# Gate and up chunks of a mixture-of-experts kernel: two row tiles of each matrix, formed side by side

## The reference

```python
def run_block(args):
    xb, e = args                       # up to 128 rows that chose expert e
    return (jax.nn.silu(xb @ w_gate[e]) * (xb @ w_up[e])) @ w_down[e]
# w_gate, w_up: (32, 1024, 512); w_down: (32, 512, 1024); two experts are chosen for each row
```

## Time and profile before

| | |
|---|---|
| median of 3 runs | 1684.39 us (1683.79 to 1686.82) |
| the profiled execution, span | 1682.9 us |
| what lies around its span (median less span) | 1.5 us |
| PE busy in the span | 96% |
| first matmul of expert 0 | 1070.8 us |
| last matmul of the experts | 1643.8 us |
| the end after it (last scatters, final norm, stores) | 39 us |

### The profile page before, as it was taken

The page is one execution under the profiler, slowest core; times in us unless marked ns, Lnnn a source line. Parts: engine busy times, 40 slices in busy tenths (PEclk is TensorE's granted clock), DMA queues, the critical chain, the costliest instruction groups (busy, mean ns, idle before and its releaser), DMA issues.

```text
span 1682.9 us, 26202 instructions
## 1 busy us (share of the span) xinstructions
PE 1613.2 (96%) x9427; PEld 1470.9 (87%) x9427; DVE 1104.4 (66%) x1967; ACT 845.3 (50%) x1234; POOL 231.8 (14%) x245
## 2 busy tenths in 40 slices
PE   5999999999999999999999999799999999999992
PEld 4999999999999999999999887688888888877781
DVE  5332588888887232114214676898998998888893
ACT  6011366666665321112112211678878778778783
POOL 1111011110110000000000111322122122232310
PEclk9999999999999999999999999799999999999996
DMA  5252111111112111131113712999999999999966
GB/s 151 72 137 79 55 51 51 50 49 39 50 50 88 30 39 50 50 137 52 50 50 126 291 71 82 357 393 379 370 377 376 380 375 379 369 373 370 361 222 224
DMA packets 131857, 305.30 MB, mean 181 GB/s; under 512 B 30404, under 2 KB 92080, under 8 KB 106936
## 3 DMA queue, kind: packets, MB, share of 16 engines
q1 hardware_dynamic: 115415, 267.76, 43.3%
q0 software_dynamic: 16384, 36.76, 7.5%
HBM read 282.81 MB, written 40.41 MB: 192 GB/s over the span
## 4 chain that ended last, share of the span: by engine, by line
PE 88%; DMA 6%; DVE 3%; issue 1%; ACT 1%; SPq 0%; DVEq 0%; POOLq 0%; ACTq 0%
PE bank L725 10%; PE bank L727 9%; PE bank L726 9%; PE bank L1071 8%; PE bank L1059 6%; PE bank L1061 6%; PE bank L1060 6%; PE bank L871 5%; PE bank L873 5%; PE bank L872 5%; DMA e_raw<-in_w_e_gate_dram 5%; PE bank L1019 2%; PE bank L1021 2%; PE bank L1023 2%; PE bank L832 2%; PE bank L1048 1%
## 5 line engine op out<-in xcount | busy, mean ns | idle before, releaser
L1967 DVE TENSOR_TENSOR e_lo<-e_raw,e_hi 128x2048 fp32r<-128x2048 f32 x192 | 433.4, 2288 | 55.4 <-ACT e_hi L1378 52.5
L1378 ACT ACTIVATE e_hi<-e_raw 128x2048 fp32r<-128x2048 f32 x192 | 364.5, 1920 | 50.0 <-DMA e_raw<-in_w_e_gate_dram 20.0
L1167 ACT ACTIVATE w_hi<-w_raw 128x1024 fp32r<-128x1024 f32 x68 | 71.6, 1054 | 325.5 <-DMA w_raw<-in_w_in_dram 182.2
L1493 DVE TENSOR_TENSOR w_lo<-w_raw,w_hi 128x1024 fp32r<-128x1024 f32 x68 | 83.2, 1223 | 203.4 <-ACT w_hi L1167 203.4
L1059 PE MATMUL bank<-e_hi,xT_hi 128*128 128x512 f32 x512 | 205.4, 401 | 3.4 <-DVE xT_lo L1978 3.4
L725 PE MATMUL bank<-h_hi,w_hi 128*128 128x344 f32 x624 | 202.5, 324 | 1.1 <-DVE h_lo L1512 1.1
L1061 PE MATMUL bank<-e_hi,xT_lo 128*128 128x512 f32 x512 | 201.5, 394 | 0.0
L1060 PE MATMUL bank<-e_lo,xT_hi 128*128 128x512 f32 x512 | 201.3, 393 | 0.0
L726 PE MATMUL bank<-h_lo,w_hi 128*128 128x344 f32 x624 | 199.6, 320 | 0.0
L727 PE MATMUL bank<-h_hi,w_lo 128*128 128x344 f32 x624 | 199.6, 320 | 0.0
L871 PE MATMUL bank<-h_hi,w_hi 128*128 128x344 f32 x576 | 190.2, 330 | 0.0
(11 more groups left out here) (351 smaller groups left out, 3164.3 us busy)
## 6 DMA issues: line engine op xcount, KB each, us to landing
e_raw<-in_w_e_gate_dram SPq DMA_DIRECT2D x64, 1024.0 KB, 19.9
e_raw<-in_w_e_up_dram SPq DMA_DIRECT2D x64, 1024.0 KB, 21.1
e_raw<-in_w_e_down_dram SPq DMA_DIRECT2D x64, 1024.0 KB, 21.6
w_raw<-in_w_in_dram SPq DMA_DIRECT2D x104, 256.0 KB, 3.3
a_spill<-y_sb POOLq DMA_DIRECT2D x8, 516.0 KB, 4.0
a_raw<-a_spill SPq DMA_DIRECT2D x2, 2064.0 KB, 12.9
x_tok<-in_x_prompt_dram SPq DMA_DIRECT2D x4, 1024.0 KB, 10.7
w_raw<-in_w_attn_out_dram SPq DMA_DIRECT2D x32, 128.0 KB, 3.0
```

The costliest lines, as they stand in the source:

```text
L1378: A.activation(e_hi[:, slot % 4, :], e_raw[slot][:, :], ACT.Copy).then_inc(e_hi_done, 1)
L1967: V.tensor_tensor(e_lo[slot][:, :], e_raw[slot][:, :], e_hi[:, slot % 4, :].bitcast(F32), ALU.subtract).then_inc(e_lo_done, 1)
```

## The change

A gate or up chunk now holds two row tiles of gate and the same two of up, side by side (`e_parts`). Its load is two transfers of 512 KB, each with 4 KB for a partition; four chunks still cover an expert. The down chunks stay as they are (one transfer of 8 KB for a partition); for slot 8 the load takes its expert from another view of the array. SP thus issues 10 transfers for an expert where it issued 6. `e_need` gives the count that ACT waits for, since some slots now take 32 for a chunk and others 16.

`chunk_gu` forms both products at once: for each row tile, and each of the three products of parts, one matmul into `bank[0]` with the gate half and one into `bank[1]` with the up half, with the same stationary operand. A chunk still has twelve matmuls of 512 columns. Both banks are complete only after chunk 3, so ACT's `silu_e` waits for the end of chunk 3 (`s + 4`) and stands behind the split of chunk 6, before `x_split`. As `bank[1]` is written from an expert's first matmul on, PE waits for `act_done` of the last expert ahead of chunk 0; the wait stood ahead of `turn_act` before.

```diff
-        def e_chunk(s):
+        def e_parts(c, e):
             if c < 4:
-                w = (w_e_gate if c < 2 else w_e_up)[0].rearrange("e (p k) f -> e p k f", p=P)
-                return w, e, slice(4 * (c % 2), 4 * (c % 2) + 4)
+                return [(w[0].rearrange("e (p k) f -> e p k f", p=P), e, slice(2 * c, 2 * c + 2)) for w in (w_e_gate, w_e_up)]
...
+        def e_need(slot, u, last=False):
+            if slot % 12 in (2, 3):
+                return u * 16 + 32
+            if slot % 12 in (8, 9):
+                return u * 16 + 16
+            return u * 32 + (16 if last else 32)
...
-                sp.dma_start(e_raw[slot][:, :].rearrange("p (k f) -> p k f", k=n),
-                             w[bass.ds(ex, 1), :, ks, :].rearrange("e p k f -> p (e k) f")).then_inc(e_loaded[slot], 16)
+                for x, (src, n) in enumerate(parts):
+                    width = 2048 // len(parts)
+                    sp.dma_start(e_raw[slot][:, width * x:width * x + width].rearrange("p (k f) -> p k f", k=n), src).then_inc(e_loaded[slot], 16)
...
-            def chunk_gu(s, slot, c, par, out):
+            def chunk_gu(s, slot, c, par):
                 pe.wait_ge(e_lo_done, s + 1)
-                for k in range(4):
-                    kk = 4 * (c % 2) + k
-                    wh, wl = e_hi[:, slot % 4, 512 * k:512 * k + 512], e_lo[slot][:, 512 * k:512 * k + 512]
-                    pe.matmul(out, xT_hi[:, par, kk, :], wh, start=kk == 0, stop=False)
-                    pe.matmul(out, xT_hi[:, par, kk, :], wl, start=False, stop=False)
-                    mm = pe.matmul(out, xT_lo[:, par, kk, :], wh, start=False, stop=kk == KT - 1)
+                for k in range(2):
+                    kk = 2 * c + k
+                    w_h, w_l = e_hi[:, slot % 4, :], e_lo[slot][:, :]
+                    for a, w, st, sp_ in ((xT_hi, w_h, kk == 0, False), (xT_hi, w_l, False, False), (xT_lo, w_h, False, kk == KT - 1)):
+                        for x in range(2):
+                            mm = pe.matmul(bank[x][:, :], a[:, par, kk, :], w[:, 1024 * x + 512 * k:1024 * x + 512 * k + 512],
+                                           start=st, stop=sp_)
...
                 if down:
                     pe.wait_ge(silu_done, e)
-                chunk_gu(s, slot, 0, par, bank[0][:, :])
+                    pe.wait_ge(act_done, e)
+                chunk_gu(s, slot, 0, par)
+                chunk_gu(s + 1, (slot + 1) % 12, 1, par)
...
                 sp_(3)
                 sp_(4)
-                silu_e(e, s + 2)
                 a_split(e - 1)
                 sp_(5)
                 sp_(6)
+                silu_e(e, s + 4)
```

More of the change, by code:

```diff
@@ L370, in program @@
         rest_done, REST_FROM = h_hi_done, 16
-        f_loaded, F_FROM = e_loaded[0:NT], 16 * 16
+        f_loaded, F_FROM = e_loaded[0:NT], [512, 512, 272, 272, 512, 512, 512, 512, 256]
         block = ctx.enter_context(nc.Block())
-        def e_chunk(s):
-            c, e = s
+        def e_parts(c, e):
             if c < 4:
-                w = (w_e_gate if c < 2 else w_e_up)[0].rearrange("e (p k) f -> e p k f", p=P)
-                return w, e, slice(4 * (c % 2), 4 * (c % 2) + 4)
-            return w_e_down[0].rearrange("e (p k) f -> e p k f", p=P), e - 1, slice(2 * (c % 2), 2 * (c % 2) + 2)
+                return [(w[0].rearrange("e (p k) f -> e p k f", p=P), e, slice(2 * c, 2 * c + 2)) for w in (w_e_gate, w_e_up)]
+            w = w_e_down[0].rearrange("e (p k) f -> e p k f", p=P)
+            return [(w, e - 1, slice(2 * (c % 2), 2 * (c % 2) + 2))]
+        def e_need(slot, u, last=False):
[4 more added lines that the diff above has]
+            return u * 32 + (16 if last else 32)
         w_in_t = w_in[0].rearrange("(k p) f -> p k f", p=P)
@@ L473, in _, with load_chunk @@
             sp.dma_start(x2[0:B8, 8, :], x_sample[:, 0, :]).then_inc(x_loaded[4], 16)
-            def load_chunk(slot, c, e, wait):
+            def load_chunk(slot, c, e, wait, pair=None):
                 if wait is not None:
                     sp.wait_ge(e_used, wait)
-                w, ex, ks = e_chunk((c, e))
-                n = ks.stop - ks.start
-                sp.dma_start(e_raw[slot][:, :].rearrange("p (k f) -> p k f", k=n),
-                             w[bass.ds(ex, 1), :, ks, :].rearrange("e p k f -> p (e k) f")).then_inc(e_loaded[slot], 16)
+                if pair is None:
+                    parts = [(w[bass.ds(ex, 1), :, ks, :].rearrange("e p k f -> p (e k) f"), ks.stop - ks.start) for w, ex, ks in e_parts(c, e)]
+                else:
+                    parts = [(w_e_down[0].rearrange("(a b) (p k) f -> a b p k f", b=2, p=P)[bass.ds(pair, 1), 0, :, 0:2, :].rearrange("e p k f -> p (e k) f"), 2)]
+                for x, (src, n) in enumerate(parts):
+                    width = 2048 // len(parts)
+                    sp.dma_start(e_raw[slot][:, width * x:width * x + width].rearrange("p (k f) -> p k f", k=n), src).then_inc(e_loaded[slot], 16)
             sp.wait_ge(chunk_out, 159)
@@ L511, in load_round @@
                         cc, de = cc + 4, de
-                    load_chunk(c, cc, i * 2 + (1 + de), i * 12 + (1 + c))
+                    load_chunk(c, cc, i * 2 + (1 + de), i * 12 + (1 + c), i + 1 if c == 8 else None)
             with sp.Fori(0, 14) as i:
@@ L1090, in step_e @@
                     pe.wait_ge(silu_done, e)
-                chunk_gu(s, slot, 0, par, bank[0][:, :])
+                    pe.wait_ge(act_done, e)
+                chunk_gu(s, slot, 0, par)
+                chunk_gu(s + 1, (slot + 1) % 12, 1, par)
                 if isinstance(e, int) and e == 0:
                     pe.wait_ge(xT_lo_done, 1)
-                chunk_gu(s + 1, (slot + 1) % 12, 1, par, bank[0][:, :])
                 if down:
                     turn_act(e - 1)
-                chunk_gu(s + 2, (slot + 2) % 12, 2, par, bank[1][:, :])
+                chunk_gu(s + 2, (slot + 2) % 12, 2, par)
                 if not down:
                     turn_x(1 - par, e + 1)
-                chunk_gu(s + 3, (slot + 3) % 12, 3, par, bank[1][:, :])
+                chunk_gu(s + 3, (slot + 3) % 12, 3, par)
                 if down and more:
@@ L1411, in step_e @@
             def step_e(e, par, s, base, uses, first=False):
-                sp_ = lambda c: e_split(s + c, (base + c) % 12, uses + 16 * ((base + c) // 12 + 1))
+                last = isinstance(e, int) and e == NE - 1
+                sp_ = lambda c: e_split(s + c, (base + c) % 12, e_need(base + c, uses + (base + c) // 12, last and c >= 6))
                 if not first:
@@ L1439, in _ @@
             for c in range(2):
-                e_split(c, c, 16)
+                e_split(c, c, e_need(c, 0))
             act.wait_ge(wsum_done, 1)
@@ L1445, in _ @@
             for c in range(2, 5):
-                e_split(c, c, 16)
-            silu_e(0, 2)
-            e_split(5, 5, 16)
+                e_split(c, c, e_need(c, 0))
+            e_split(5, 5, e_need(5, 0))
             x_split(1, 1)
-            e_split(6, 6, 16)
+            e_split(6, 6, e_need(6, 0))
+            silu_e(0, 4)
             step_e(1, 1, 4, 4, 0, first=True)
@@ L1453, in _ @@
             with act.Fori(1, 15) as i:
-                step_e(i * 2 + 1, 1, i * 12 + 4, 4, i * 16)
-                step_e(i * 2 + 2, 0, i * 12 + 10, 10, i * 16)
-            step_e(31, 1, 184, 4, 240)
+                step_e(i * 2 + 1, 1, i * 12 + 4, 4, i)
+                step_e(i * 2 + 2, 0, i * 12 + 10, 10, i)
+            step_e(31, 1, 184, 4, 15)
             a_split(31)
@@ L1479, in _ @@
                 rows = P if n < 8 else B8
-                act.wait_ge(f_loaded[n], F_FROM + 16)
+                act.wait_ge(f_loaded[n], F_FROM[n] + 16)
                 A.activation(f_junk[0:rows, :], f_out[0:rows, n, :], ACT.Square, accum_out=ssq[0:rows, n:n + 1]).then_inc(f_sq, 1)
```

## The result

| | before | after |
|---|---|---|
| median | 1684.5 us (4 runs) | 1701.8 us (4 runs, 1695.3 to 1704.15) |
| ratio, 95% interval | | 1.0093 [1.0077, 1.0109] |
| span of the profiled execution | 1682.9 us | 1702.6 us |

The change costs 17.3 us (by the interval 13.0 to 18.4). The forecast was 1698.1, slower, in a range of 1686 to 1709. Direction and range hold. Of the working, the stream that bounds and the price of the shorter pieces hold; two terms that it put at nothing do not, and that the sum comes so near is in part luck.

A forecast was written before the change was run, and what follows sets the result against it. PE was taken to bound first, the DMA stream with its slow engines from about 1460 on. Profiled 1682.9 us plus 13.7 for shorter pieces, other terms zero, gave 1696.6, with 1.5 around it 1698.1; range 1686 to 1709.

The forecast's parts named there:

- Bound: Expert loop: PE sets the pace until the loads' lead is used up, from about 1460 on the DMA stream.
- The last stretch: Sign at the end, when only the last loads are on their way: the engines' share of 0.28 stays.
- Part 1: Gate and up loads of experts 2 to 31: 4 KB pieces cost 114 ns a chunk, 13.7 us over 120 chunks.
- Rivals A: 4 KB pieces in the loads: only a small fixed cost, 27 ns a chunk, 3.2 us, giving 1687.6; chance 0.12.
- B: Loads: no cost, slow engines' delay comes from bytes, gathers and scatters alone; 1684.4 us; chance 0.12.
- C: Loads: faster, short pieces share engines better with gathers and scatters, PE's 5 us of waits end; 1679.4; chance 0.07.
- Part 2: SP's queue: issuing 10 transfers an expert where it issued 6 costs nothing, as long as SP isn't held up.
- rival D: SP held up by near 150 queued pieces per engine: 0.3 us an expert, 9 us on top, 1707; chance 0.09.
- Part 3: PE's gate and up matmuls: same number and size, at most 0.1 us an expert, counted as zero.
- Part 4: Later silu on ACT and PE's moved wait ahead of chunk 0, with 3.7 us to spare: zero.
- No PE wait names `act_sb` first: Sign of a right forecast: after the change, no wait of PE has DVE's `act_sb` as its first cause.
- A clock below 1.00 in the experts, which I exclude: Sign of a wrong forecast, excluded because the clock stayed at 1.00 with PE at 132.63 of 136 us.

The follow-up runs named there:

- loads_halved: Kernel before, each gate or up chunk loaded by two 512 KB transfers of 4 KB pieces, products and waits unchanged: 1695.2 us, ratio 1.0064.
- one_dma_4k: Kernel before, each gate or up chunk of experts 1 to 31 as one 1 MB transfer in 4 KB pieces: 1697.8 us, ratio 1.0079.
- before_late9: Kernel before, at most nine chunks of loads on their way in place of twelve, from the fifth round of twelve chunks on: 1686.2 us, ratio 1.0008.
- after_spread: Changed kernel, each expert's rows spread over all 128 partitions: 1680.05 us, ratio to before 0.9973.
- order_only: Changed kernel's products, silu and waits, but each chunk loaded as one transfer of 8 KB pieces as in before: 1690.5 us, ratio to before 1.0034.
- the changed kernel with banks 2 and 3: Changed kernel, expert 0's gate and up products in banks 2 and 3, no wait ahead of expert 1: 1697.7 us; with rows spread too, 1677.2 us.
- halved_late9: Kernel before with gate and up loads halved into 4 KB pieces, lead of nine chunks from the fifth round on: 1692.4 us, ratio 1.0045.
- before_spread: Kernel before, each expert's rows spread over all 128 partitions by another table of slots: 1676.9 us, ratio 0.9954.

## Why the prediction was right, and where it wasn't

Bound: right. The time is that of the DMA stream from the expert on at which the lead is used up, and its slow engines decide. PE is never idle from 1110 to 1360 and waits first in 1360 to 1380, some 12 experts after 1150, as the text had it. The landing times stop rising earlier, from 1300 on, and at 24 us rather than 27; that fits that a part of the wait then lies in SP's issues. The last 17 experts take 18.9 us each (320.9 / 17), where it had 19.0. PE is busy for 130.96 of 136 us, 96.3% (below 97%). The last stretch, taken as far from the end as the one of the earlier trace rows, has a share of 0.37 (0.28 before), about as said, though 2 us earlier it is 0.51. The packets are as forecast: in 1056 to 1062 q1 moves 2.38 MB at 99.6% of the engines, 581 pieces of 4 KB at 165 ns.

Part 1, 4 KB pieces, +13.7 us: right in mechanism and somewhat too large. The runs give 10.2 and 12.8 us, 85 and 107 ns a chunk in place of 114; these include 3 us or so of SP's held-up issues, so the pieces alone cost 7 to 10. The rates don't explain why it is less: the purest window (403 against 425 GB/s) gives 135 ns a chunk, 16 us. This stays open. What the text did not have is that the price is one of the slow engines only; with the rows spread it is nothing that can be measured. Rivals A, B and C are excluded, as loads_halved alone is 7.8 us slower than before at the lower end of its interval.

The rule of the Trainium skill that the prediction cites (DMA: Bandwidth & Descriptors, "Why small descriptors are slow (HBM only)") gives 3.5 us by its estimate. The runs' 7 to 10 us for the pieces alone are two to three times that.

Part 2, nothing "as long as SP isn't held up": SP is held up, as rival D had it, and this term is not nothing. The issues go from 0.33 up to 6.2 us. By the prediction's estimate ten loads of 8 KB pieces stand for 90 pieces on each engine, with 0.33 us an issue; 4 KB pieces would make that about 150, and SP is held up on the way there. It is the pieces and not the ten issues (one_dma_4k has six). The price is likely some 3 us and not 9, which fits that the lead above nine chunks buys little in the steady stretch (before_late9, +1.0).

Part 3, PE: right. after has PE at 17.9 us an expert from expert 2 to 14, as before.

Part 4, silu and the moved wait, "Zero": this is the step that failed most plainly, and it is worth 3 to 5.5 us (2.9 with even engines, 4.1 and 5.5 without). The text read its 3.7 us to spare in an expert of the middle, and there it holds: after has only one PE wait that names `act_sb` ahead of line 1070 in all 32 experts. But what hides it is the down product of the expert before (24 matmuls, 5.5 us), and between the products of expert 0 and those of expert 1 there is none. There the whole chain lies bare: the end of chunk 3, a table load of 1.28 us, silu 0.60, `act_sb` 1.06, and the ways between them, 3.49 us in all. The reading was taken in the loop; the first pass, which the code writes out (`if down`), has no such product, and the prediction says nothing of it. "No PE wait names `act_sb` first" was thereby wrong, once, and once was enough.

"A clock below 1.00 in the experts, which I exclude": wrong too. The reason given spoke of the stretch in which loads are late; the idle time at expert 0 wasn't in it. In the profiled execution of after the lower clock cost 2.5 us more. Whether it follows this idle time differs from execution to execution: it did in after and after_spread, and not in order_only. That this is why after's runs lie as far apart as 1695.3 and 1704.15 is likely but only argued; the mean clock over the span is 0.984 in the first of these, as in before, and 0.980 to 0.982 in the other three.

The sum is closer than its parts, and that is luck: 5.5 us of order and wait were missing, and 13.7 stood for loads that cost 10.2. Had only the loads been changed, 1698 would have been 3 us too high; as it is, it is 4 too low.

Open: 17.3 - 15.7 = 1.6 us are within the scatter of the runs. The size of the queue at which SP is held up is known only to lie above what ten 8 KB loads put into it.

## What to carry to other kernels

Where a moved wait is free only because other work covers it, look for the pass in which the cover is missing, the first and the last one above all: here a single stop at the start was kept to the end, and the transfers, which ran short later, had stood still with it. Before a stream of transfers is made finer or coarser, see whether all engines carry the same: evening them out took 8.1 us off before, and 20.5 us off the changed kernel with banks 2 and 3 (1697.7 to 1677.2), the whole price of its short pieces included. A transfer's landing time is to be read together with the time of its issue, since a full queue moves waiting from one into the other.

## What the runs showed of the hardware

- SP's issue isn't of constant length. It takes 0.33 us for before's chunks (median), with some 90 pieces queued for each engine by the prediction's estimate, and up to 6.2 us (after) and 7.4 us (one_dma_4k) with 4 KB pieces and a lead of twelve chunks, be it ten transfers an expert or six. With a lead of nine it is 0.33 us again (median, halved_late9). In before's first 5 us, behind many short pieces, one took 8.10 us.
- With all engines full, 4 KB pieces ran at 403 and 404 GB/s (one_dma_4k and after, 1056 to 1062) and 8 KB pieces at 425 and 423 (before, before_spread). Over 120 MB this was worth an estimated 7 to 10 us where the stream bounds, and nothing measurable where it doesn't.
- Beside gathers and scatters of some 64 rows of 4 KB on neighbouring partitions, loads of weights landed after up to 28.8 us. With the rows spread over all partitions (before_spread), those issued from 1100 on landed after 9.7 us at most, with the engines' mean share the same (1.00 in 1464 to 1600).
- An idle time of PE of 3.49 us (after) and one of 3.48 us (after_spread) were followed by a granted clock of 0.50; one of 3.48 us in order_only was not. The Trainium skill (TensorE: Matmul & The Clock Gate, "HAM oscillation — how this bites in real kernels") has waits of PE for data between groups of matmuls as what brings the lower clock; the first two executions agree, the third doesn't.
